# Expert rows stored from the unscaled residual, the norm's factor moved to a scale per slot, and SyncE's first expert loads issued around the first gather

## The chip, the cores and the metric

The kernel runs on one core of one Trainium2 chip. The metric is the time of one execution in device microseconds; a comparison takes the median of several. The five engines that matter here are TensorE (PE, with its weight loads PEld), VectorE (DVE), ScalarE (ACT), GpSimd (POOL) and SyncE (SP). SP, ACT and POOL also issue DMAs.

## What is computed

A two-layer model on 512 tokens of width 1024, float32 throughout. Each layer is a mixer, a cross attention and a mixture of experts, each added to the residual `h`. The change lies in the experts alone:

```python
def hier_moe(xn, w_grp, b_grp, w_exp, b_exp, w1, w3, w2):       # xn = rmsnorm(h, gain)
    ...                                   # router: a group of 4, then the best 2 of its 4 experts, w_tok
    gate = jnp.sum(jax.nn.one_hot(eid, N_EXPERTS) * w_tok[..., None], axis=1)
    hid = jax.nn.silu(jnp.einsum('td,edf->tef', t, w1)) * jnp.einsum('td,edf->tef', t, w3)
    hid = hid * gate[..., None]
    y = hid.reshape(t.shape[0], N_EXPERTS * EXP_FF) @ w2.reshape(N_EXPERTS * EXP_FF, dm)
```

`rmsnorm(h, g)` is `h * rstd * g`, with one `rstd` per token. There are 16 experts, w1 and w3 are 1024 x 256, w2 is 256 x 1024.

## The kernel before

Every engine runs one hand-written program; the order on an engine is the order of its code, and engines meet at semaphores. A layer's experts work on items: an item is one expert with 128 slots for token rows. With these inputs there are 16 items in a layer, four quads of four.

**The rows.** After the cross attention `h` lies in SBUF as four tiles of 128 tokens. ACT's `norm` squares each tile (L1466), then `experts` on ACT scales it by `rstd` into `xn` (L1723, in the buffer `E`) and stores it to the DRAM tensor `xs` (L1727). The semaphore `xs_stored` counts these four stores. POOL gathers an item's rows from `xs` by an indirect DMA (L699) into one of two buffers, PE turns them (L1153), and ACT and DVE split them into high and low parts (L1751, L2423). Item 0 takes another way: PE picks its rows out of `xn` with a one-hot matrix (`first_rows`, L1115).

**The router.** DVE computes it in one long row of small instructions (L2295 to L2398), most of which wait for the one before. In it are the slots of each token (`slots_ready`, on which POOL's first gather waits), the gates (L2368, L2369), and a one-hot product that brings the gates to the slots (`item_gate`, L2370 and L2372, PE's L1137, and the copy L2398 to `gslot`). Behind it DVE splits item 1's up weights (L2412) and rows (L2419, L2423); PE's `up` of item 1 (L1175, then L1185) needs them.

**An item.** `up` (both up projections in one 512-column bank), `turn_hidden` (L1197), `turn` (L1153, of the rows two items ahead) and `down` (L1214) on PE; on ACT the silu L1756, the high parts of the weights (L1743, L1763), and the copies of the result to `yo` (L1795); on DVE the product with the gate (L2404) and the low parts. ACT takes an item's up weights (L1743) two items before PE uses them.

**The loads.** SP loads the weights: `load_up` (2048 KB, L542) and `load_down` (1024 KB, L545) into four slots each, and stores the results of items 0 to 12 to `ybuf` (L551); all are on SP's one DMA queue. For items 0 to 3 the order is written out; from item 4 on a load waits until its slot is free. In layer 0 the queue ends with a 2048 KB panel of layer 1 and the store of item 12. Then POOL gathers rows of `ybuf` back into `h` (L726, eight times, adding), DVE adds the last three items, which PE brings to tokens (L1237, added at L2478), and layer 1 starts with PE turning `h` (L783).

Of the kernel before, what the change touches and what calls it, by code (L numbers as in the profile page):

```python
# [28 lines left out]
ALU = mybir.AluOpType  # L29
# [49 lines left out]
def program(nc, A, out):  # L79
# [19 lines left out]
    with ctx:  # L99
# [226 lines left out]
        xn = v3(E[0], 4)  # L326

# [136 lines left out]
        item_gates = st[:, 232:236]  # L464
# [29 lines left out]
        def c3(ap):  # L494
# [15 lines left out]
        item_gate = v3(E4, 8, 1536, 1536 + 8 * NI)  # L510
        LATE = 3
        slot_of_row, tile_row, late_tok, gslot = [
            sm[:, lo:lo + n] for lo, n in ((592, 4 * LATE), (604, 4), (611, LATE), (616, NI))]
# [12 lines left out]
        def _(sp):  # L526
# [8 lines left out]
            def experts(l):  # L535
# [19 lines left out]
                for j in range(2):  # L555
                    load_up(NE * l + j, j)
                    load_down(NE * l + j, j)
                    if j == 0:
                        sp.wait_ge(S["xs_stored"], 16 * TT * (l + 1))
                load_up(NE * l + 2, 2)  # L560
                await_filled(sp, first[f"route{l}"])
                load_down(NE * l + 2, 2)
                sp.wait_ge(m["xt_filled"], 2)
                sp.wait_ge(m["xg_in1"], 16)
# [59 lines left out]
        def _(pool):  # L624
# [56 lines left out]
            def experts(l):  # L681
# [7 lines left out]
                def gather(q, j):  # L689

                    par = j % 2
                    if not isinstance(q, int) or j >= 2:

                        wait_alone(m["xt_filled"], q * (2 * SLOTS) + (2 * j - 2))
                    if not isinstance(q, int):
                        pool.tensor_copy(item_gates[:, j:j + 1], gslot[:, bass.ds(q * SLOTS + j, 1)])  # L696
                    pool.tensor_copy(idx[:, par:par + 1], slots[:, bass.ds(q * SLOTS + j, 1)]).then_inc(m["idx_ready"], 1)
                    wait_alone(m["idx_ready"], q * SLOTS + j)
                    pool.indirect_dma_start(xg[par], None, xs[l],  # L699
                                            bass.IndirectOffsetOnAxis(ap=idx[:, par:par + 1], axis=0),  # L700
                                            bounds_check=T - 1, oob_is_err=False)\
                        .then_inc(m[f"xg_in{par}"], 16)
# [70 lines left out]
        def _(pe):  # L773
# [300 lines left out]
            def experts(l):  # L1074
# [33 lines left out]
                pe.wait_ge(S["xs_rows"], TT * (l + 1))  # L1108
# [3 lines left out]
                def first_rows(b, k0, k1):  # L1112
                    for k in range(k0, k1):
                        for t in range(TT):
                            ins = pe.matmul(banks[b][:, k * P:(k + 1) * P], xn[:, t, (4 * b + k) * P:(4 * b + k + 1) * P],  # L1115
                                            first1h[:, t, :], start=(t == 0), stop=(t == TT - 1))
                    if k1 == 4:
                        ins.then_inc(m["xt_filled"], 1)
# [12 lines left out]
                def slot_gates():  # L1131

                    u = first[f"gslot{l}"]
                    claim(pe, u)
                    pe.wait_ge(S["onehots_ready"], 2 * l + 2)
                    for n in range(2 * TT):
                        ins = pe.matmul(bank(u)[:, 0:NI], slot1h[:, n, :].bitcast(F32), item_gate[:, n, :], start=(n == 0),  # L1137
                                        stop=(n == 2 * TT - 1))
                    fill(ins, u)
# [281 lines left out]
        def _(act):  # L1421
# [34 lines left out]
            def squares(name, t0=0, t1=TT):  # L1456

                n = NORMS[name]
                for t in range(t0, t1):
                    h_is_ready(name, t)  # L1460
                    if name == "mix_norm0":
                        dst = memV[:, t % MT, :]
                        act.wait_ge(S["stat_ready"], t + 1)
                    else:
                        dst = E[3 if name == "mix_norm1" else 1][:, t * D:(t + 1) * D]
# [251 lines left out]
            def experts(l):  # L1717
                m = M[l]
                norm(f"ffn_norm{l}")
                act.wait_ge(S["rstd_ready"], 3 * l + 2)  # L1720
                for t in range(TT + 1):
                    if t < TT:
                        act.activation(xn[:, t, :], h[:, t, :], ACT.Copy,  # L1723
                                       scale=rstd[:, NORMS[f"ffn_norm{l}"], t:t + 1]).then_inc(S["xs_rows"], 1)
                    if t > 0:
                        act.wait_ge(S["xs_rows"], TT * l + t)
                        act.dma_start(xs[l][(t - 1) * P:t * P, :], xn[:, t - 1, :]).then_inc(S["xs_stored"], 16)  # L1727
# [25 lines left out]
                def gated_hidden(q, j):  # L1753

                    act.wait_ge(m["hid_filled"], q * SLOTS + (j + 1))
                    act.activation(silu[j % 2], banks[2 + j % 2][:, 0:FF], ACT.Silu).then_inc(m["silu_ready"], 1)  # L1756
# [216 lines left out]
        def _(dve):  # L1973
# [306 lines left out]
            def experts(l):  # L2280
# [89 lines left out]
                v(tt(item_gate, mid(iof[:, 0:NI], 8), last(itemf, NI), ALU.is_equal))  # L2370
                gates = gate[:, :, :].rearrange("p j t -> p (j t)")
                v(tt(item_gate, item_gate, last(gates, NI), ALU.mult), "onehots_ready")  # L2372
# [25 lines left out]
                evac(dve.tensor_copy(gslot, bank(u)[:, 0:NI]), u)  # L2398

                def hidden(q, j):  # L2400
                    par = j % 2
                    dve.wait_ge(m["silu_ready"], q * SLOTS + (j + 1))
                    gate_ = gslot[:, j:j + 1] if isinstance(q, int) else item_gates[:, j % SLOTS:j % SLOTS + 1]
                    stt(hid[par], silu[par], gate_, banks[2 + par][:, FF:2 * FF], ALU.mult, ALU.mult).then_inc(m["hid_ready"], 1)  # L2404
# [370 lines left out]
```

## Time and profile before

| | |
|---|---|
| median of 3 runs | 1171.49 us (1171.18 to 1172.44) |
| the profiled execution | 1168.69 us, span 1166.9 us |
| busy shares of the span | PE 97%, DVE 62%, ACT 57%, POOL 31% |
| granted TensorE clock, mean | 0.990 |
| experts, layer 0 | from 378 us to 575 us of the span |
| experts, layer 1 | from 965 us to the end |

The page's shares are means over very different stages. In the experts one item takes 9.87 us, and in that stretch PE, DVE, ACT and the DMA engines are all busy over 90% of the time. So the views to read are those that show order: the chain that ended last, the timelines of PE and SP at the start of the experts, and the time from a DMA's issue to its landing. The start of the experts in layer 1 repeats that of layer 0 about 587 us later.

### The profile page before, as it was taken

The numbers are of one execution on the slowest core, as the hardware profiler recorded it, in microseconds if no ns is written. First come the engines' busy times: TensorE is split into PE (matmuls) and PEld (weight loads), VectorE is DVE, ScalarE is ACT, GpSimd is POOL, SyncE is SP. The second block draws the span as 40 slices with busy tenths as digits, with TensorE's granted clock in tenths as the row PEclk, the third lists the DMA queues.
The fourth block names the chain that finished last, engine by engine and source line by source line (L and its number), as shares of the span: only waits on it lengthen the run. The fifth ranks groups of instructions, "written<-read, shape, count | busy, mean of one in ns | idle before, by whom it ended". The sixth has DMA issues, their size and how long they took to land.

```text
span 1166.9 us, 15858 instructions
## 1 busy us (share of the span) xinstructions
PE 1131.8 (97%) x5330; PEld 868.5 (74%) x5330; DVE 726.6 (62%) x1315; ACT 661.0 (57%) x1275; POOL 367.2 (31%) x343
## 2 busy tenths in 40 slices
PE   9998999999999899999999999989999998999998
PEld 5467875788778567777878887668887786677776
DVE  5896444322332899999644993682313408999996
ACT  2553256345542489999625354444365524799993
POOL 2033350564223011111636654253442130111104
PEclk9998899999999999999999999999999999999999
DMA  9524031278100999997722120011311008999968
GB/s 377 216 112 102 12 118 73 90 277 354 73 1 7 366 396 405 399 395 283 175 87 81 73 106 39 1 73 73 142 75 73 1 1 323 389 402 393 392 273 191
DMA packets 35413, 216.38 MB, mean 185 GB/s; under 512 B 9499, under 2 KB 9627, under 8 KB 23296
## 3 DMA queue, kind: packets, MB, share of 16 engines
q1 hardware_dynamic: 23024, 181.02, 40.0%
q0 software_dynamic: 9888, 27.17, 8.0%
q10 hardware_dynamic: 2432, 7.29, 1.6%
q8 instruction: 41, 0.67, 0.2%
q14 instruction: 28, 0.23, 0.1%
HBM read 191.31 MB, written 32.51 MB: 192 GB/s over the span
## 4 chain that ended last, share of the span: by engine, by line
PE 81%; DVE 11%; DMA 3%; ACT 3%; issue 2%; SPq 0%; DVEq 0%; ACTq 0%
PE bank L832 39%; PE bank L1185 12%; PE bank L1214 8%; DMA E<-in_xt 2%; PE bank L1033 2%; PE bank L1055 2%; PE bank L1175 2%; PE bank L1237 2%; PE bank L805 1%; PE bank L994 1%; PE bank L937 1%; DVE E L2088 1%; DVE E2r L2438 1%; DVE E L2086 1%; DVE E L2087 1%
## 5 line engine op out<-in xcount | busy, mean ns | idle before, releaser
L661 POOL TENSOR_TENSOR wlo<-W,whi 128x512 fp32r<-128x512 f32 x176 | 257.1, 1481 | 422.6 <-ACT whi L1444 422.1
L1444 ACT ACTIVATE whi<-W 128x512 fp32r<-128x512 f32 x176 | 108.5, 631 | 240.4 <-PE bank L832 236.3
L832 PE MATMUL bank<-whi,xTr 128*128 128x512 f32 x480 | 193.5, 403 | 0.9 <-ACT E L1936 0.7
L832 PE MATMUL bank<-wlo,xTr 128*128 128x512 f32 x416 | 162.8, 391 | 0.0
L832 PEld LDWEIGHTS bank<-whi,xTr 128*128 128x128 f32 x480 | 90.7, 189 | 22.0 <-POOL wlo L661 1.7
L1185 PE MATMUL bank<-E4r,E1r 128*128 128x512 f32 x360 | 99.9, 426 | 0.0
L832 PE MATMUL bank<-whi,E4r 128*128 128x512 f32 x256 | 99.8, 390 | 0.0
L2038 DVE TENSOR_TENSOR h<-bank,h 128x512 f32<-128x512 f32 x32 | 21.8, 692 | 115.0 <-PE bank L832 115.0
L832 PEld LDWEIGHTS bank<-wlo,xTr 128*128 128x128 f32 x416 | 78.7, 189 | 16.7 <-issue 1.2
L1185 PEld LDWEIGHTS bank<-E4r,E1r 128*128 128x128 f32 x360 | 67.6, 188 | 27.6 <-issue 8.5
L1214 PE MATMUL bank<-whi,E2r 128*128 128x512 f32 x240 | 82.2, 404 | 3.5 <-DVE E2r L2438 1.8
L832 PE MATMUL bank<-whi,E0r 128*128 128x512 f32 x160 | 63.7, 398 | 0.0
L832 PE MATMUL bank<-whi,E2r 128*128 128x512 f32 x160 | 62.4, 390 | 0.0
L832 PE MATMUL bank<-wlo,E0r 128*128 128x512 f32 x160 | 62.2, 389 | 0.0
L696 POOL COPY st<-sm 128x1 f32 x24 | 4.4, 183 | 180.1 <-PE bank L1153 180.1
L1214 PEld LDWEIGHTS bank<-whi,E2r 128*128 128x128 f32 x240 | 45.0, 188 | 19.5 <-DVE E2r L2438 11.0
L832 PEld LDWEIGHTS bank<-whi,E4r 128*128 128x128 f32 x256 | 48.0, 188 | 10.0
L856 PE MATMUL bank<-W,E 128*128 128x512 f32 x128 | 55.4, 593 | 0.0
L1214 PE MATMUL bank<-wlo,E2r 128*128 128x512 f32 x120 | 46.8, 390 | 0.0
L856 PEld LDWEIGHTS bank<-W,E 128*128 128x128 f32 x128 | 24.2, 190 | 29.7 <-issue 29.2
L2412 DVE SCALAR_TENSOR_TENSOR E4r<-E,vectors,E4r 128x512 fp32r<-128x512 f32 x64 | 45.1, 748 | 0.0
L726 POOL DMA_INDIRECT h<-ybuf,pos x16 | 32.0, 1997 | 41.9 <-DMA ybuf<-E 37.6
(497 smaller groups left out, 2566.5 us busy)
## 6 DMA issues: line engine op xcount, KB each, us to landing
W<-in_panels SPq DMA_DIRECT2D x25, 2048.0 KB, 8.2
W<-in_up SPq DMA_DIRECT2D x16, 2048.0 KB, 13.2
E<-in_up SPq DMA_DIRECT2D x16, 2048.0 KB, 14.1
E<-in_down SPq DMA_DIRECT2D x16, 1024.0 KB, 14.7
xT<-in_down SPq DMA_DIRECT2D x16, 1024.0 KB, 15.4
ybuf<-E SPq DMA_DIRECT2D x26, 512.0 KB, 9.6
ybuf<-memV POOLq DMA_DIRECT2D x12, 1024.0 KB, 22.7
h<-in_x SPq DMA_DIRECT2D x8, 512.0 KB, 12.8
```

What stands on the lines that cost most here:

```text
L661: pool.tensor_tensor(wlo[s_ % RING][:, :], slot(name)[:, block_of(name, k), :], whi[s_ % RING][:, :].bitcast(F32), ALU.subtract).then_inc( ...
L726: pool.indirect_dma_start(h[:, t, :], None, ybuf[l], bass.IndirectOffsetOnAxis(ap=pos[:, j, t:t + 1], axis=0), bounds_check=NI * P - 1, oo ...
L832: ins = pe.matmul(bank(u + t)[:, :], a, b, start=(k == 0 and n == 0), stop=(k == KT - 1 and n == 2))
L856: ins = pe.matmul(bank(u)[:, :], memnT[:, k, t * P:(t + 1) * P], slot(f"kv{n}")[:, k, :], start=(k == 0), stop=(k == KT - 1))
L1033: ins = pe.matmul(bank(u)[:, head * NM:(head + 1) * NM], qT[:, k, t * P:(t + 1) * P], memKT[:, k, :], start=(kk == 0), stop=(kk == 1))
L1055: ins = pe.matmul(bank(u)[:, :], memV[:, k, n * XD + d * P:n * XD + (d + 1) * P], pT[:, n, k, :], start=(k == 0), stop=(k == 1))
L1175: pe.matmul(banks[2 + par][:, :], xgT[:, k, :], w13s[j][:, k, :], start=(k == 0), stop=False)
L1185: ins = pe.matmul(banks[2 + par][:, :], a, b, start=False, stop=(c == SPLIT - 1 and n == 2))
L1214: ins = pe.matmul(banks[5 + half][:, :], a, b[:, :], start=(k == 0 and n == 0), stop=(k == 1 and n == 2))
L1237: ins = pe.matmul(banks[b][:, :], late1h[:, n, t * P:(t + 1) * P], y[:, half * 512:(half + 1) * 512], start=(n == 0 and part == 0), stop=( ...
L1444: act.activation(whi[s_ % RING][:, :], slot(name)[:, block_of(name, k), :], ACT.Copy).then_inc(S["w_hi"], 1)
L2412: stt(up_lo[c], w13s[nj][:, k, :], col("norm_ffn_g", 8 * l + k), up_hi[c].bitcast(F32), ALU.mult, ALU.subtract).then_inc(m["lo_parts"], 1)
```

## The change

- `norm` on ACT now stores each tile of `h` to `xs` as soon as the tile is ready, ahead of its square. The four scalings of L1723, the buffer `xn` and the stores behind them are gone. `first_rows` on PE reads `h`.
- The rows of an item are now unscaled. Where they were scaled by `rstd`, the silu takes `rstd` of its slot as its scale, and the gate of a slot becomes gate times `rstd`. DVE builds both per token and item (`item_scale`), PE brings both to the slots in one product of 48 columns where there were 24, and `scale_of` picks the column.
- SP's first loads, written out for items 0 to 3, stand in another order and behind other waits.

```diff
                 sp.wait_ge(S["spare_rows"], 16 * 2 * (NI - NE + SLOTS) * P // NM)
-                for j in range(2):
-                    load_up(NE * l + j, j)
-                    load_down(NE * l + j, j)
-                    if j == 0:
-                        sp.wait_ge(S["xs_stored"], 16 * TT * (l + 1))
+                sp.wait_ge(S["xs_stored"], 16 * TT * (l + 1))
+                load_up(NE * l, 0)
+                load_up(NE * l + 1, 1)
+                load_down(NE * l, 0)
+                sp.wait_ge(m["xt_filled"], 2)
+                sp.wait_ge(m["xg_in1"], 16)
                 load_up(NE * l + 2, 2)
+                load_down(NE * l + 1, 1)
                 await_filled(sp, first[f"route{l}"])
                 load_down(NE * l + 2, 2)
-                sp.wait_ge(m["xt_filled"], 2)
-                sp.wait_ge(m["xg_in1"], 16)
                 load_up(NE * l + 3, 3)
                 load_down(NE * l + 3, 3)
...
                     h_is_ready(name, t)
+                    if "ffn" in name:
+                        act.dma_start(xs[int(name[-1])][t * P:(t + 1) * P, :], h[:, t, :]).then_inc(S["xs_stored"], 16)
...
-                act.wait_ge(S["rstd_ready"], 3 * l + 2)
-                for t in range(TT + 1):
-                    if t < TT:
-                        act.activation(xn[:, t, :], h[:, t, :], ACT.Copy,
-                                       scale=rstd[:, NORMS[f"ffn_norm{l}"], t:t + 1]).then_inc(S["xs_rows"], 1)
-                    if t > 0:
-                        act.wait_ge(S["xs_rows"], TT * l + t)
-                        act.dma_start(xs[l][(t - 1) * P:t * P, :], xn[:, t - 1, :]).then_inc(S["xs_stored"], 16)
...
-                    act.activation(silu[j % 2], banks[2 + j % 2][:, 0:FF], ACT.Silu).then_inc(m["silu_ready"], 1)
+                    act.activation(silu[j % 2], banks[2 + j % 2][:, 0:FF], ACT.Silu, scale=scale_of(q, j, 1)).then_inc(m["silu_ready"], 1)
...
-                v(tt(item_gate, mid(iof[:, 0:NI], 8), last(itemf, NI), ALU.is_equal))
+                row_rstd = rstd[:, NORMS[f"ffn_norm{l}"], :]
+                v(tt(gate[:, :, :], gate[:, :, :], mid(row_rstd, 2), ALU.mult))
+                v(tt(item_scale[:, :, 1, :], mid(iof[:, 0:NI], 8), last(itemf, NI), ALU.is_equal))
                 gates = gate[:, :, :].rearrange("p j t -> p (j t)")
-                v(tt(item_gate, item_gate, last(gates, NI), ALU.mult), "onehots_ready")
+                v(tt(item_scale[:, :, 0, :], item_scale[:, :, 1, :], last(gates, NI), ALU.mult))
+                for j in range(2):
+                    half = item_scale[:, TT * j:TT * (j + 1), 1, :]
+                    ins = tt(half, half, last(row_rstd, NI), ALU.mult)
+                v(ins, "onehots_ready")
```

On SP, where the experts of layer 0 begin (`W` and `E` with `in_up` are the slots of the up weights, `E` and `xT` with `in_down` those of the down weights), the order before was:

```order
L542 DMA W<-in_up 128x4096 [waits filled6,spare_rows,filled2]
L545 DMA E<-in_down 128x2048
L542 DMA W<-in_up 128x4096 [waits xs_stored]
L545 DMA E<-in_down 128x2048
L542 DMA E<-in_up 128x4096
L545 DMA xT<-in_down 128x2048 [waits filled7]
L542 DMA E<-in_up 128x4096 [waits xg_in1_0,xt_filled_0]
L545 DMA xT<-in_down 128x2048
```

On SP, the same eight loads after:

```order
L546 DMA W<-in_up 128x4096 [waits spare_rows,filled6,xs_stored,filled2]
L546 DMA W<-in_up 128x4096
L549 DMA E<-in_down 128x2048
L546 DMA E<-in_up 128x4096 [waits xg_in1_0,xt_filled_0]
L549 DMA E<-in_down 128x2048
L549 DMA xT<-in_down 128x2048 [waits filled7]
L546 DMA E<-in_up 128x4096
L549 DMA xT<-in_down 128x2048
```

Six loads stood ahead of the wait for the first gather's landing (`xg_in1`), now three do; the five behind it are item 2's up, item 1's and 2's down, and item 3's pair. The wait for the rows' stores (`xs_stored`) now stands ahead of all of them.

On DVE, in the router where the gates are ready (`gate` holds them, `E` the one-hots per item), the order before was:

```order
L2368 TENSOR_TENSOR gate<-sm 128x4 [waits d_step]
L2369 TENSOR_TENSOR gate<-gate,sm 128x4 [waits d_step]
L2370 TENSOR_TENSOR E<-iof,E 128x192 [waits d_step]
L2372 TENSOR_TENSOR E<-E,gate 128x192 [waits d_step]
L2374 COPY E<-iof 1x48 [waits onehots_ready]
```

On DVE, the same place after:

```order
L2366 TENSOR_TENSOR gate<-sm 128x4 [waits d_step]
L2367 TENSOR_TENSOR gate<-gate,sm 128x4 [waits d_step]
L2369 TENSOR_TENSOR gate<-gate,rstd 128x8 [waits d_step]
L2370 TENSOR_TENSOR E<-iof,E 128x8x24 [waits d_step]
L2372 TENSOR_TENSOR E<-E,gate 128x8x24 [waits d_step]
L2375 TENSOR_TENSOR E<-E,rstd 128x4x24 [waits d_step]
L2375 TENSOR_TENSOR E<-E,rstd 128x4x24
L2378 COPY E<-iof 1x48 [waits onehots_ready]
```

Three instructions are new, one of 8 columns and two of 96; nothing on DVE is taken away.

## Rows read from the trace of the kernel before

**Rows 1.** Chain that ended last, layer 0: start us, us, what.

```profile
399.66 0.69 DVE E L2286
...
412.40 0.48 DVE E1r L2423
...
412.92 1.12 PE bank L1175 x2
```

**Rows 2.** Timeline of PE: start us, us, instructions, [idle before, what ended it].

```profile
410.21 1.09 PE L1153 MATMUL bank<-ident,E 128*128 128x128 f32 x8 [0.88 <-DMA E<-xs,idx]
...
997.99 1.09 PE L1153 MATMUL bank<-ident,E 128*128 128x128 f32 x8 [1.66 <-DMA E<-xs,idx]
1000.07 1.13 PE L1175 MATMUL bank<-W,E 128*128 128x512 f32 x2 [0.99 <-DVE E1r L2423]
```

**Rows 3.** Timelines of DVE and ACT at the start of the experts, layer 0.

```profile
376.51 1.06 ACT L1466 ACTIVATE E<-h 128x1024 f32<-128x1024 f32 x1 [7.48 <-DVE h L2038]
383.92 0.34 ACTq L1727 DMA_DIRECT2D xs<-E  x1
381.02 0.16 DVE L1986 TENSOR_SCALAR ssq<-ssq 128x4 f32<-128x4 f32 x1
386.22 0.24 DVE L2305 TENSOR_TENSOR sm<-sm,vectors 128x80 f32<-128x80 f32 x1
```

**Rows 4.** Groups of instructions on ACT, shapes apart: count, busy us, mean ns.

```profile
L1743 ACT ACTIVATE E4r<-E,vectors 128x512 fp32r<-128x512 f32 x64 | 42.8, 723 | 0.0
L1763 ACT ACTIVATE whi<-E 128x512 fp32r<-128x512 f32 x64 | 35.1, 634 | 0.0
```

**Rows 5.** Timelines of SP and POOL: issues of the first loads and of the first gather.

```profile
393.66 0.33 SPq L542 DMA_DIRECT2D W<-in_up  x1
394.51 0.43 SPq L542 DMA_DIRECT2D E<-in_up  x1
400.27 1.10 POOL L699 DMA_INDIRECT E<-xs,idx  x1 [0.98 <-PE bank L1115]
```

**Rows 6.** Issue to landing, us: item 1's down, item 2's up, the first gather (layer 0).

```profile
L545 SPq DMA_DIRECT2D E<-in_down x1: 434/434/434, 394.0 to 394.0; - x1
DMA to landing us min/median/max: 9.7/9.7/9.7
DMA to landing us min/median/max: 14.7/14.7/14.7
DMA to landing us min/median/max: 9.9/9.9/9.9
```

**Rows 7.** Issue to landing, us: eight gathers L726 of layer 0; final stores of `h`.

```profile
DMA to landing us min/median/max: 5.9/7.0/8.1
DMA to landing us min/median/max: 2.6/3.6/4.4
```

**Rows 8.** By stage: us; PE, PEld, DVE, ACT, POOL busy; clock, DMA share, GB/s.

```profile
503.00:513.00 10.00, 9.94 (x47) 7.78 (x46) 9.50 (x17) 9.16 (x18) 1.33 (x3) 1.00 0.99 399
546.00:548.00 2.00, 2.00 (x15) 1.72 (x14) 2.00 (x4) 1.16 (x4) 0.00 (x0) 1.00 0.13 53
```

**Rows 9.** Layer 1: landing of item 6's up; item 15's up; ACT's first use of it.

```profile
DMA to landing us min/median/max: 13.4/13.4/13.4
L542 SPq DMA_DIRECT2D E<-in_up x1: 341/341/341, 1111.6 to 1111.6; - x1
DMA to landing us min/median/max: 18.6/18.6/18.6
1131.85 1.95 ACT L1743 ACTIVATE E4r<-E,vectors 128x512 fp32r<-128x512 f32 x3
```

**Rows 10.** Timelines of POOL, DVE and PE at the end of layer 0's experts.

```profile
550.50 1.58 POOL L726 DMA_INDIRECT h<-ybuf,pos  x1 [19.41 <-DMA ybuf<-E]
573.17 1.29 DVE L2478 TENSOR_TENSOR h<-bank,h 128x512 f32<-128x512 f32 x2 [0.91 <-DMA h<-ybuf,pos]
575.26 3.65 PE L783 MATMUL bank<-ident,h 128*128 128x128 f32 x32
```

More of the change, by code:

```diff
@@ L324, in v3 @@
             return buf[:, lo:hi].rearrange("p (a b) -> p a b", a=a)
-        xn = v3(E[0], 4)
         s5T = v3(E[0], G)
@@ L463, in program @@
         xmx, xnm, xsum, xrec = st[:, 0:16], st[:, 16:32], st[:, 32:48], st[:, 48:64]
-        item_gates = st[:, 232:236]
         wsN = v3(wsT, 4)
@@ L509, in program, with scale_of @@
         half_ = E4[:, 1920:1924]
-        item_gate = v3(E4, 8, 1536, 1536 + 8 * NI)
+        item_scale = E4[:, 3072:3072 + 16 * NI].rearrange("p (n a i) -> p n a i", n=8, a=2)
+        slot_scales = v3(sm, 2, 520, 520 + 2 * NI)
+        item_scales = v3(st, 2, 232, 232 + 8)
+        def scale_of(q, j, a):
+            return slot_scales[:, a, j:j + 1] if isinstance(q, int) else item_scales[:, a, j % 4:j % 4 + 1]
         LATE = 3
-        slot_of_row, tile_row, late_tok, gslot = [
-            sm[:, lo:lo + n] for lo, n in ((592, 4 * LATE), (604, 4), (611, LATE), (616, NI))]
+        slot_of_row, tile_row, late_tok = [
+            sm[:, lo:lo + n] for lo, n in ((592, 4 * LATE), (604, 4), (611, LATE))]
         nquad, late_from, past = E4[:, 296:297], E4[:, 297:298], E4[:, 304:312]
@@ L695, in gather @@
                     if not isinstance(q, int):
-                        pool.tensor_copy(item_gates[:, j:j + 1], gslot[:, bass.ds(q * SLOTS + j, 1)])
+                        pool.tensor_copy(item_scales[:, :, j:j + 1], slot_scales[:, :, bass.ds(q * SLOTS + j, 1)])
                     pool.tensor_copy(idx[:, par:par + 1], slots[:, bass.ds(q * SLOTS + j, 1)]).then_inc(m["idx_ready"], 1)
@@ L1107, in experts @@
                     taken(pe, max(v for v in range(u + 1) if bank_of[v] == b))
-                pe.wait_ge(S["xs_rows"], TT * (l + 1))
                 fill_wait(unused, memory_keys, 1)
@@ L1114, in first_rows @@
                         for t in range(TT):
-                            ins = pe.matmul(banks[b][:, k * P:(k + 1) * P], xn[:, t, (4 * b + k) * P:(4 * b + k + 1) * P],
+                            ins = pe.matmul(banks[b][:, k * P:(k + 1) * P], h[:, t, (4 * b + k) * P:(4 * b + k + 1) * P],
                                             first1h[:, t, :], start=(t == 0), stop=(t == TT - 1))
@@ L1136, in slot_gates @@
                     for n in range(2 * TT):
-                        ins = pe.matmul(bank(u)[:, 0:NI], slot1h[:, n, :].bitcast(F32), item_gate[:, n, :], start=(n == 0),
+                        ins = pe.matmul(bank(u)[:, 0:2 * NI], slot1h[:, n, :].bitcast(F32),
+                                        item_scale[:, n, :, :].rearrange("p a i -> p (a i)"), start=(n == 0),
                                         stop=(n == 2 * TT - 1))
@@ L2397, in experts @@
                 await_filled(dve, u)
-                evac(dve.tensor_copy(gslot, bank(u)[:, 0:NI]), u)
+                evac(dve.tensor_copy(slot_scales, bank(u)[:, 0:2 * NI].rearrange("p (a i) -> p a i", a=2)), u)
                 def hidden(q, j):
@@ L2402, in hidden @@
                     dve.wait_ge(m["silu_ready"], q * SLOTS + (j + 1))
-                    gate_ = gslot[:, j:j + 1] if isinstance(q, int) else item_gates[:, j % SLOTS:j % SLOTS + 1]
-                    stt(hid[par], silu[par], gate_, banks[2 + par][:, FF:2 * FF], ALU.mult, ALU.mult).then_inc(m["hid_ready"], 1)
+                    stt(hid[par], silu[par], scale_of(q, j, 0), banks[2 + par][:, FF:2 * FF], ALU.mult, ALU.mult).then_inc(m["hid_ready"], 1)
                 def up_low_parts(q, j, c0, c1, part):
```

## The prediction

> **What bounds the kernel now.** I read the chain that ended last first, in the two places where the experts begin, then PE's timeline there. Between the router and item 1's `up` the chain is one engine's: DVE runs from L2286 at 399.66 us to the first half of L2423 at 412.40, with nothing on the chain between but its own next instruction, and PE's L1175 starts at 412.92 the moment DVE lets it [rows 1]. PE also waits for the first gather there, 0.88 us in layer 0 and 1.66 us in layer 1 [rows 2], but what follows that gather still waits for DVE. To be seen in these rows: the wait that the change shortens, for the gather, is not the one that ends last.
>
> Then I read the stages. Inside the experts a stretch of 10 us has PE busy 9.94, DVE 9.50, ACT 9.16, and a DMA share of 0.99 at 399 GB/s [rows 8]. PE sets the pace there, but the DMA engines have nothing to spare. That is why I read the landing times last, and they decide: in layer 1 item 6's up weights land 13.4 us after their issue, item 15's 18.6 us after [rows 9]. The issues keep PE's pace, so the landings fall behind by 5.2 us in nine items, about 0.6 us for each. The queue never catches up, and whatever delay it starts with it carries to the end.
>
> **The change part by part. The rows' store.** ACT loses four scalings, and PE a wait on them that had long been met. None is on the chain, so they are worth nothing. The four issues move ahead of the squares. One took 0.34 us [rows 3]; the first stands open before the first square, the others run beside the square before them. The DVE instruction that waits for the squares started at 381.02 [rows 3], right behind DVE's own earlier work, so I take 0.2 us for a later route, with 0 and 0.35 as ends.
>
> **The scale per slot.** DVE gains one 8-column and two 96-column instructions in the chain of rows 1. A small one of the same engine took 0.16 us, an 80-column one 0.24 [rows 3]. With the step to the next instruction that makes 0.2 + 2 x 0.25 = 0.7 us per layer, 0.4 if the two run into each other, 0.8 at most. PE's product has 48 columns for 24, inside `first_up`, which ends before DVE is ready: nothing. The silu's scale becomes a column of SBUF. On ACT 512 columns took 0.723 us with such a scale and 0.634 without [rows 4], so 0.09 us per item, under an engine that is not full [rows 8]; where the last quad's chain goes through the silu it may show, 0 to 0.2 us per layer. POOL copies two columns for one: nothing. Together these make 0.7 + 0.2 = 0.9 us per layer at most places, less where one hides the other; I carry 0.85, or 1.7 us for both layers.
>
> **The loads.** Here is the large term. Before, SP restarted at 393.66 with item 1's up, and item 1's down, item 2's up and down stood right behind it [rows 5]. After, the rows are stored where the squares began, at 376.5, where their stores had begun at 383.9 [rows 3], and item 0's up, item 1's up and item 0's down follow them at about 385 us (2.1 MB of stores are 5 us at the 400 GB/s of rows 8, and some 3 us pass from issue to landing, rows 7): 5.2 MB, another 13 us. They are in before the first gather is issued at 400.27 [rows 5], so nothing that needs them waits: item 1's up comes earlier than before, item 0's down is first used once item 1's `up` runs. But the next five loads now wait until that gather has landed, and behind them on SP stand item 4's loads and all stores and loads after them. Between, the DMA engines have only the gather to move.
>
> How long is that? Under load the first gather took 9.9 us [rows 6]. On idle engines no row shows it. From below, the plain 512 KB stores at the kernel's end took 2.6 to 4.4 us, 3.6 in the middle; from above, the adding gathers of 128 full rows took 5.9 at least [rows 7]. I take 4.0, near the plain stores, as the rows are plain copies and fewer, with POOL's 1.10 us for the instruction [rows 5] in it. The gather then lands at 404.3, and the queue restarts there instead of at 393.66: 10.6 us later. It has one up and the gather less to move. Item 1's down landed at 394.03 + 9.7 = 403.7 and item 2's up at 394.51 + 14.7 = 409.2 [rows 5, 6], so an up beside the gather takes 5.5 us. **The lag is 10.6 - 5.5 = 5.1 us**, with 3.7 and 7.0 as ends (2.6 and 5.9 for the gather). Layer 1 repeats this stretch 587.15 us later (PE's L1175 at 1000.07 and 412.92) [rows 1, 2], so I take the same lag.
>
> The Trainium skill, "DMA: Bandwidth & Descriptors", section "Anatomy of one DMA — SWDGE (gpsimd) path", gives about 2.0 us plus the bytes at 436 GB/s for one DMA. For 512 KB that is an estimate of 3.2 us by that page, which the final stores bear out (2.6 to 4.4, rows 7). With it the lag would be 4.3 and the sum below 6.2 us instead of 7.8.
>
> Where does the lag come out? In layer 0 the last store is at the queue's very end. POOL waited 19.41 us for it and began at 550.50; between 546 and 548 only 0.13 of the DMA engines was still at work [rows 8, 10], so it is a few of them that finish late. Through the gathers into `h` the third tile's add ended at 573.17 + 1.29 = 574.46, having waited for its gather, and PE's L783 starts at 575.26 [rows 10]: 0.8 us of room. Layer 0 loses 5.1 - 0.8 = 4.3 us. In layer 1 item 15's up landed at 1111.6 + 18.6 = 1130.2 and ACT first read it at 1131.85 [rows 9]: 1.65 us of room, so 5.1 - 1.65 = 3.45 us, by which ACT, DVE and PE stop in the last quad. The 0.85 us of DVE in each layer lie under these: they move PE, while the loads' landing stays where it is.
>
> **Sum:** 4.3 + 3.45 = 7.75 us on the profiled 1168.69, so 1176.4. The runs shown have a median 2.8 us above that execution, so I predict 1171.49 + 7.8 = **1179.3 us**. The ends of the lag give 2.9 + 2.05 = 4.95 and 6.2 + 5.35 = 11.55 us, or 1176.4 and 1183.0.
>
> **The rivals. The lag is absorbed.** The loads of a layer are issued by free slots, and if the engines that finish late were idle at some time before the tail, the lag would end there. For it: the room of items 4 to 12 is larger than that of item 15, and the overall share of 0.99 is a mean over 16 engines. Against it: the growth of rows 9. Then only DVE's 1.7 us remain: 1173.2 us, 0.5 to 2.5 above before. This is the case of no change.
>
> **The gather's wait was the bound.** Then PE gets back 0.88 + 1.66 us, and in layer 1 the 0.99 us that follow [rows 2], 3.5 us in all: 1168.0 us, faster. It needs DVE to be free earlier; but L2412 and L2423 stand in a fixed order behind the router on DVE, and the chain has no gap for another to fill [rows 1]. It decides only if DVE's stretch shrinks by more than the 0.7 us added, for which I see no reason.
>
> **The gather stays slow.** If the three loads are still in the queue at 400 us, because the stores land late, the gather again takes up to 9.9 us [rows 6]. The lag is then 400.27 + 9.9 - 393.66 - 5.5 = 11.0 us, and the two layers lose 10.2 + 9.35 = 19.6: 1191.1 us. For it: four stores of 512 KB and three loads in some 23 us is close. Against it: they make 7.3 MB, 18 us at 400 GB/s.
>
> **How the numbers follow.** Forecast 0.62 (1176.4 to 1183.0), absorbed 0.20, gather was the bound 0.08, gather stays slow 0.10. Everything within 0.2% of before (2.3 us, about what a measurement of this kernel tells from no change) comes from the absorbed case, 0.17; its upper part, the forecast and the slow gather make slower 0.74; the gather case and a little of the absorbed one make faster 0.09. The range goes from 1172.0, the lower end of the absorbed case, to 1183.0; it leaves out the two last rivals, 0.18.
>
> **What would show it.** In the changed trace item 2's up should be issued near 404 us, and the first gather land in about 4 us. PE's wait before its first L1153 should be gone, and L1175 of item 1 should start 0.7 to 1 us later, released by DVE. The landing of item 15's up should be later by the lag in both layers, with a wait of ACT on it in layer 1; POOL's first L726 of layer 0 should start near 555.6, and DVE's L2478 wait for gathers before L783. I am wrong if the lag at item 4 is there but gone by item 12, or if item 1's `up` starts earlier than before.

## The result

The kernel after takes 1177.31 us in the median of 20 runs (1170.39 to 1185.05), the kernel before 1171.39 us of as many on the same chip: a ratio of 1.0068 on record, interval 1.0045 to 1.009, or 5.3 to 10.5 us more (the two medians alone give 1.0051, or 5.9 us). Forecast were 7.8 us more, and 1179.3.

Every kernel here, the one before included, varies over 7 to 16 us from run to run, and the longer runs have the lower mean granted clock (of before, some 0.987 at 1172 us and 0.995 at 1163 us). Unchanged stretches show it; here are two windows before the experts, first of before, then of after (us; PE, PEld, DVE, ACT, POOL busy; clock, DMA share, GB/s):

```profile
100.00:120.00 20.00, 18.18 (x126) 17.02 (x124) 6.60 (x12) 7.41 (x14) 2.42 (x2) 0.75 0.60 108
120.00:140.00 20.00, 20.00 (x74) 15.48 (x74) 7.95 (x7) 4.69 (x8) 5.19 (x3) 0.82 0.02 4
```

```profile
100.00:120.00 20.00, 18.18 (x153) 16.47 (x152) 6.61 (x12) 7.53 (x14) 2.49 (x3) 1.00 0.61 113
120.00:140.00 20.00, 20.00 (x82) 15.22 (x81) 15.78 (x10) 6.09 (x11) 13.04 (x5) 1.00 0.02 4
```

The profiled execution of after came 7.65 us sooner to the experts, through code that the change does not touch, so its span (1170.3 against 1166.9) understates the loss. I therefore count each layer from ACT's first square of the experts' norm. In before that is at 376.51 [rows 3] and in layer 1 at 963.51; in after at 368.86 and 962.61, the first row being before's, the others after's (ACT timelines):

```profile
963.51 1.06 ACT L1466 ACTIVATE E<-h 128x1024 f32<-128x1024 f32 x1 [7.48 <-DVE h L2038]
```

```profile
368.86 1.06 ACT L1472 ACTIVATE E<-h 128x1024 f32<-128x1024 f32 x1 [7.86 <-DVE h L2036]
962.61 1.06 ACT L1472 ACTIVATE E<-h 128x1024 f32<-128x1024 f32 x1 [7.85 <-DVE h L2036]
```

From there layer 0 ends (PE's last turn of `h`) at 202.40 in before (575.26 + 3.65, [rows 10]) and 207.32 in after (574.43 + 1.75, below): **4.92 us more**. Layer 1 takes 203.39 to the end of the span in before and 207.69 in after: **4.30 us more**. Between the layers, in unchanged code, after took 1.83 us longer: PE stood still for 2.79 us at 784 us of the span, and the clock behind it was 0.62 for 3 us, where before kept 1.00 behind the same pause of 2.86 us. The sum is 4.92 + 4.30 + 1.83 - 7.65 = 3.4, the difference of the spans.

### The profile page after: what moved, and what is told of

It is laid out like the page before. It is cut to its first block, busy times and chain, and to the rows that moved or that the text cites. A ratio compares the mean times of both kernels' runs of the same rounds, so it can differ in the third digit from the quotient of the medians.

```text
span 1170.3 us, 15854 instructions
## 1 busy us (share of the span) xinstructions
PE 1128.9 (96%) x5330; PEld 863.8 (74%) x5330; DVE 728.4 (62%) x1321; ACT 655.2 (56%) x1267; POOL 366.6 (31%) x343
## 4 chain that ended last, share of the span: by engine, by line
PE 69%; DVE 13%; ACT 6%; DMA 6%; issue 4%; POOL 0%; SPq 0%; ACTq 0%; DVEq 0%; POOLq 0%
PE bank L836 39%; PE bank L1189 7%; PE bank L1218 4%; DMA E<-in_xt 2%; PE bank L1037 2%; PE bank L1059 2%; DMA h<-ybuf,pos 2%; DVE E4r L2415 2%; DVE wlo L2435 2%; ACT uhi L1741 1%; PE bank L1179 1%; PE bank L809 1%; PE bank L998 1%; DVE E L2086 1%; ACT E L1793 1%
## 5 line engine op out<-in xcount | busy, mean ns | idle before, releaser
L1189 PE MATMUL bank<-E4r,E1r 128*128 128x512 f32 x360 | 102.9, 436 | 0.0
L700 POOL COPY st<-sm 128x2 f32 x24 | 4.5, 186 | 187.1 <-PE bank L1157 187.1
L1741 ACT ACTIVATE E4r<-W,vectors 128x512 fp32r<-128x512 f32 x56 | 37.2, 722 | 15.7 <-DVE sm L2402 15.7
```

What stands on the lines that cost most here:

```text
L1189: ins = pe.matmul(banks[2 + par][:, :], a, b, start=False, stop=(c == SPLIT - 1 and n == 2))
L1741: act.activation(up_hi[c], w13s[nj][:, NATIVE + c, :], ACT.Copy, scale=col("norm_ffn_g", 8 * l + NATIVE + c))\
```

## The profile after

PE where item 1 begins, first in before's layer 0, then in after's layer 0 and layer 1 (timeline; answers to [rows 2]), and after's windows around that place in layer 0:

```profile
412.92 1.12 PE L1175 MATMUL bank<-W,E 128*128 128x512 f32 x2 [1.62 <-DVE E1r L2423]
```

```profile
401.32 1.04 PE L1157 MATMUL bank<-ident,E 128*128 128x128 f32 x8
405.89 1.69 PE L1179 MATMUL bank<-W,E 128*128 128x512 f32 x2 [3.53 <-DVE E1r L2426]
406.60 4.80 PE L1189 MATMUL bank<-E4r,E1r 128*128 128x512 f32 x12
...
999.76 1.64 PE L1179 MATMUL bank<-W,E 128*128 128x512 f32 x2 [3.66 <-DVE E1r L2426]
```

```profile
398.00:402.00 4.00, 4.00 (x21) 2.52 (x21) 3.54 (x14) 1.49 (x3) 0.00 (x0) 1.00 0.88 295
402.00:405.80 3.80, 0.36 (x4) 0.12 (x2) 3.80 (x8) 3.77 (x7) 2.16 (x3) 1.00 0.92 377
405.80:408.80 3.00, 2.91 (x6) 1.75 (x7) 3.00 (x7) 1.99 (x4) 0.00 (x0) 0.59 1.00 422
408.80:412.00 3.20, 3.20 (x14) 2.59 (x13) 2.37 (x4) 2.14 (x3) 0.00 (x0) 0.85 1.07 451
```

PE no longer waits for the gather. But the wait for DVE that was 1.62 us in before is now 3.53 us in one piece, and behind it the clock is 0.59 for 3 us, so most of that window is at its lower level of 1.2 GHz: L1179 takes 1.69 us for 1.12. That I had not foreseen.

The transfers, issue to landing in us. Layer 0's last store in before:

```profile
542.97 0.35 SPq L551 DMA_DIRECT2D ybuf<-E  x1
DMA to landing us min/median/max: 6.6/6.6/6.6
```

In after the first gather of layer 0 and of layer 1, item 2's up, layer 0's last store, and item 15's up in layer 1:

```profile
DMA to landing us min/median/max: 4.1/4.1/4.1
DMA to landing us min/median/max: 4.2/4.2/4.2
...
396.62 0.33 SPq L546 DMA_DIRECT2D E<-in_up  x1
DMA to landing us min/median/max: 9.9/9.9/9.9
...
L555 SPq DMA_DIRECT2D ybuf<-E x1: 351/351/351, 538.0 to 538.0; - x1
DMA to landing us min/median/max: 9.9/9.9/9.9
...
L546 SPq DMA_DIRECT2D E<-in_up x1: 341/341/341, 1113.0 to 1113.0; - x1
DMA to landing us min/median/max: 19.5/19.5/19.5
```

The gather lands in 4.1 us, against 9.9 [rows 6]. The last store lands at 547.9, 179.0 us behind the first square; in before it landed at 549.6, 173.1 behind. **The lag at the queue's end is 5.9 us.**

What it does to layer 0's end (timelines of DVE and PE; answers to [rows 10]), and DVE's waits in layer 1's last third, first in before, then in after (us in total, times, longest):

```profile
566.87 1.29 DVE L2481 TENSOR_TENSOR h<-bank,h 128x512 f32<-128x512 f32 x2 [4.21 <-DMA h<-ybuf,pos]
573.09 1.29 DVE L2481 TENSOR_TENSOR h<-bank,h 128x512 f32<-128x512 f32 x2 [1.20 <-DMA h<-ybuf,pos]
572.04 2.16 PE L787 MATMUL bank<-ident,h 128*128 128x128 f32 x18 [1.68 <-DVE h L2481]
574.43 1.75 PE L787 MATMUL bank<-ident,h 128*128 128x128 f32 x14 [0.24 <-DVE h L2481]
```

```profile
DVE h L2478 <- PE bank L1237: 4.0, 3, 1.4
```

```profile
DVE h L2481 <- DMA h<-ybuf,pos: 5.5, 4, 2.2
```

In both layers DVE's last adds now wait for gathers into `h`, and in layer 0 PE for them; in before those of layer 1 waited for PE.

## The experiments

Times below are counted from the layer's first square, in each kernel's profiled execution: the start of item 1's `up`, the turn of item 0's hidden rows (L1197 before, L1201 after), the end of the layer. The ratios are to the kernel before on the same chip. One execution gives each row's layer times, so they need not add up to its ratio: they do within the interval, but for e2's and e3's: these lose 12.2 and 8.2 us in the two layers, where their intervals end at 11.8 and 7.4 us.

| kernel | layer 0: up, hidden, end | layer 1: up, hidden, end | median us | ratio (interval) |
|---|---|---|---|---|
| before | 36.41, 42.23, 202.40 | 36.56, 42.38, 203.39 | | |
| after | 37.03, 44.47, 207.32 | 37.15, 44.57, 207.69 | 1177.31 | 1.0068 (1.0045 to 1.009) |
| e1, old order | 37.04, 44.38, 204.60 | 37.17, 45.89, 206.99 | 1175.09 | 1.0044 (1.0011 to 1.0077) |
| e2, new order alone | 36.42, 43.84, 209.65 | 37.60, 45.01, 208.34 | 1175.21 | 1.0068 (1.0034 to 1.0101) |
| e3, free loads | 37.05, 45.56, 206.77 | 37.37, 46.05, 207.17 | 1173.67 | 1.0031 (0.9999 to 1.0063) |
| e4, six products | 38.49, 44.21, 206.49 | 38.49, 44.18, 205.55 | 1177.77 | 1.0054 (1.0024 to 1.0084) |
| e5, three products | 37.04, 42.86, 208.53 | 37.16, 42.98, 204.68 | 1173.39 | 1.005 (1.0021 to 1.0078) |
| e6, old order, two products | 37.04, 42.85, 203.02 | 37.16, 43.00, 204.08 | 1168.25 | 1.000 (0.9972 to 1.0027) |
| e7, second gather awaited | 37.04, 42.85, 209.20 | 37.18, 42.96, 205.65 | 1175.14 | 1.008 (1.0052 to 1.0107) |
| e8, free loads, three products | 37.04, 42.85, 203.40 | 37.18, 42.96, 204.00 | 1168.00 | 1.0003 (0.9975 to 1.0031) |
| e9, doubled lag | 37.04, 42.86, 212.08 | 37.16, 42.97, 208.81 | 1176.78 | 1.0101 (1.0059 to 1.0143) |
| e10, table on POOL | 36.04, 41.83, 202.34 | 36.04, 41.83, 203.09 | 1165.97 | 0.9982 (0.9954 to 1.001) |

### One part at a time: e1, e2, e3

The theory was the prediction's: the lag of SP's queue carries the loss. The rival: the scale per slot does. **e1** gives the changed kernel SP's old order:

```diff
-                sp.wait_ge(S["xs_stored"], 16 * TT * (l + 1))
-                load_up(NE * l, 0)
-                load_up(NE * l + 1, 1)
-                load_down(NE * l, 0)
-                sp.wait_ge(m["xt_filled"], 2)
-                sp.wait_ge(m["xg_in1"], 16)
-                load_up(NE * l + 2, 2)
-                load_down(NE * l + 1, 1)
+                for j in range(2):
+                    load_up(NE * l + j, j)
+                    load_down(NE * l + j, j)
+                    if j == 0:
+                        sp.wait_ge(S["xs_stored"], 16 * TT * (l + 1))
+                load_up(NE * l + 2, 2)
                 await_filled(sp, first[f"route{l}"])
                 load_down(NE * l + 2, 2)
+                sp.wait_ge(m["xt_filled"], 2)
+                sp.wait_ge(m["xg_in1"], 16)
                 load_up(NE * l + 3, 3)
```

> The changed kernel with SP's eight first loads in the order and behind the waits of before; the stores of h and the scale per slot stay. Theory (the lag of SP's queue carries the loss): item 2's up is issued near 386 us less than 1 us behind before, item 4's up and the last store land within 1 us of before, the first POOL gather into h starts within 1 us of before, and only DVE's 0.8 us per layer is left, so the median is 0 to 1.7 us above before. Rival (the scale on DVE and ACT is the loss): the median stays where the changed kernel's is, about 6 to 8 us above before. With the loads under the gather again, PE's idle time before item 1's up should be in two pieces and the granted clock behind it 1.00.

The lag was gone (layer 0's last store at 172.4), yet layer 0 ended 2.2 us and layer 1 3.6 us behind before: neither theory. PE's rows of both layers, and the window there in layer 1, tell why:

```profile
412.49 2.08 PE L1179 MATMUL bank<-W,E 128*128 128x512 f32 x2 [3.04 <-DVE E1r L2426]
...
1003.48 2.08 PE L1179 MATMUL bank<-W,E 128*128 128x512 f32 x2 [2.51 <-DVE E1r L2426]
```

```profile
1003.40:1010.40 7.00, 6.92 (x16) 4.78 (x17) 5.13 (x10) 4.23 (x7) 0.39 (x2) 0.55 1.02 428
```

Ahead of these waits PE had waited for the gather too, 0.28 us in layer 0 and 0.93 in layer 1:

```profile
408.36 1.09 PE L1157 MATMUL bank<-ident,E 128*128 128x128 f32 x8 [0.28 <-DMA E<-xs,idx]
...
999.87 1.09 PE L1157 MATMUL bank<-ident,E 128*128 128x128 f32 x8 [0.93 <-DMA E<-xs,idx]
```

So the idle time was in two pieces, as in before, but the longer one was 3.04 and 2.51 us where before's was 1.62 and 1.66: the gather landed 0.8 to 1.0 us sooner, and DVE came 0.6 us later. The clock behind it was 0.55 in layer 1, and L1179 took 2.08 us for 1.12 in both. My expectation of a clock of 1.00 was wrong, and the whole loss of layer 1 stands already at item 0's hidden rows (45.89 against 42.38).

**e2** is the kernel before with the changed order of SP, the reverse of the diff above:

> The kernel before with SP's eight first loads in the order and behind the waits of the change, nothing else; the stores still follow the four scalings. Theory (the lag carries the loss): the queue restarts when the first gather has landed, some 10 us later than before, and the median is 4 to 9 us above before; somewhat more than in the changed kernel if the loads ahead of the gather, which wait for later stores here, still slow the gather. Rival (the scale is the loss): within 1 us of before.

The order alone costs as much as the whole change: 7.25 us in layer 0, 4.95 in layer 1. A part of the 7.25 us is a second pause, at the layer's end: PE waited there 3.77 us for DVE and the gathers, and turned `h` in 5.32 us for 3.65. The scale isn't in this kernel, and the lower clock is there all the same:

```profile
411.54 1.50 PE L1175 MATMUL bank<-W,E 128*128 128x512 f32 x2 [2.73 <-DVE E1r L2423]
```

So the lower clock does not need the scale; that it comes from PE's idle time is what e4 and e5 test.

**e3** moves the wait for the gather three loads back, with the early stores kept:

```diff
                 load_down(NE * l, 0)
-                sp.wait_ge(m["xt_filled"], 2)
-                sp.wait_ge(m["xg_in1"], 16)
                 load_up(NE * l + 2, 2)
                 load_down(NE * l + 1, 1)
                 await_filled(sp, first[f"route{l}"])
                 load_down(NE * l + 2, 2)
+                sp.wait_ge(m["xt_filled"], 2)
+                sp.wait_ge(m["xg_in1"], 16)
                 load_up(NE * l + 3, 3)
```

> The changed kernel with item 2's up and items 1's and 2's down ahead of the wait for the first gather, as many loads ahead of it as before, but all behind the early stores of h. Theory (lag): the queue starts earlier than before's and has no gap, so the loads from item 4 on land no later than before's, and the median is 1 us below to 1.7 us above before. The gather is slow again (8 to 10 us), so if the early gather was what matters (rival), the loss or gain should show at item 1's up: later than in the changed kernel by 1 us or more and the median above before by 2 us or more.

The first store of results lands at 54.3, 2.1 us ahead of before's, and the gather at 32.0, as slow as expected; item 1's `up` starts where after's does, so the early gather bought nothing. But PE's idle time is 3.54 us, and its clock is lower for longer than in after: the hidden rows come 3.33 us behind before. The leading loads could not help a PE that was late itself.

### The clock by itself: e4, e5, e6, e8

**e4** fills PE's idle time, in the changed kernel, with products into a bank that nothing uses there:

```diff
                 first_up()
                 turn(0, 1)
+                fill_wait(5, memory_keys, 6)
```

> The changed kernel with six more products of 128x512 on PE into an unused bank (0.54 us each) between the turn of item 1's rows and its up, where PE is idle for 3.5 us. Rival (the lower granted clock behind that idle time is the loss): item 1's up goes from 7.4 to 5.8 us, and the median falls by 2 to 3.5 us, 1.6 us per layer. Theory (lag): the loads land where they did, so in layer 0 nothing comes of it, in layer 1 0 to 1.6 us: the median falls by 0 to 1.6 us.

Six were too many (PE timeline): each product is two passes, and together they took 5.32 us and delayed the `up` by 1.4 us.

```profile
410.17 5.32 PE L815 MATMUL bank<-memKT,ident 128*128 128x512 f32 x12
415.32 1.02 PE L1179 MATMUL bank<-W,E 128*128 128x512 f32 x2
```

Yet the `up` was fast again, and item 0's hidden rows came 0.26 us ahead of after's. Layer 1 gained 2.1 us; the medians can't tell (a ratio of 1.0054, for 1.0068 of after). **e5** has three products:

> The changed kernel with three more products of 128x512 on PE (0.89 us each, as the run with six showed) between the turn of item 1's rows and its up, so that the idle time of 3.5 us is filled by 2.7 and the up isn't delayed. Theory (two costs that don't add in layer 0: the lag of the loads and the lower granted clock): item 1's up starts as in the changed kernel, 37.0 us behind the first square, at a granted clock of 1.00, and item 0's hidden rows are turned 0.6 us behind before's instead of 2.2. Layer 0 still ends 4 to 5 us behind before, since the gathers into h end it; layer 1 ends 0.6 to 2.7 us behind before instead of 4.3. Rival (the lag alone, in both layers): layer 1's end stays 4 us behind.

PE's rows in layer 0, then DVE's waits in the last adds of layer 0 and of layer 1:

```profile
402.11 2.74 PE L815 MATMUL bank<-memKT,ident 128*128 128x512 f32 x6
405.82 1.12 PE L1179 MATMUL bank<-W,E 128*128 128x512 f32 x2 [0.96 <-DVE E1r L2427]
```

```profile
DVE h L2482 <- DMA h<-ybuf,pos: 8.3, 4, 5.6
...
DVE h L2482 <- PE bank L1241: 4.0, 3, 1.4
```

This separates the causes. The `up` starts where it did and is at full clock; hidden rows come 1.6 us sooner in both layers. Layer 1 gains 3.0 us and ends 1.29 behind before, as expected. Layer 0 ends 6.1 us behind before, where I had expected 4 to 5. Its adds wait 8.3 us for gathers, and DVE's last add ends 205.6 us behind the square, as in after (205.5), so the lag sets that. But PE, early and then idle in one piece, turns `h` slowly:

```profile
571.96 5.35 PE L787 MATMUL bank<-ident,h 128*128 128x128 f32 x32 [3.29 <-DVE h L2482]
```

Before's turn took 3.65 us [rows 10]. In e5 it ends 2.9 us behind DVE's last add, in after, whose PE had waited 1.68 us, 1.8: some 1.1 us of e5's layer 0 are the clock again (0.70 over 3 us there). **e6** is e1 with two products:

> The changed kernel with SP's loads in the order of before, and two products of 128x512 on PE (1.8 us) in the idle time of 2.5 to 3.0 us ahead of item 1's up. Theory: with the lag undone and the clock kept, only DVE's 0.6 us per layer is left; layer 0 ends 0.6 us behind before, layer 1 0.6 us, and the median is 1 to 2 us above before. Rival (something else in the scale per slot costs time in the items): both layers stay 2 us or more behind.

Both layers come out 0.62 and 0.69 us behind before, the ratio is 1.000, and DVE's adds wait for PE as in before's layer 1. That is DVE's part of the change, and nothing of the scale is left over. e5 and e6 differ in SP's order and in one product, and their items run within 0.4 us of each other in layer 0; so the two show how far a lag is carried. e5's loads land 7.0 us after e6's at item 2, 5.1 at item 4, 7.2 at item 15, and the last store 5.9 (178.7 against 172.8 behind the square; its issue and landing in e5, then in e6):

```profile
L555 SPq DMA_DIRECT2D ybuf<-E x1: 350/350/350, 536.3 to 536.3; - x1
DMA to landing us min/median/max: 11.2/11.2/11.2
```

```profile
L555 SPq DMA_DIRECT2D ybuf<-E x1: 350/350/350, 544.0 to 544.0; - x1
DMA to landing us min/median/max: 5.6/5.6/5.6
```

Over 130 us nothing of it is made up: 5 to 7 us throughout. In layer 1 the loads come as late, 5.2 us at item 2, 8.2 at item 4 and 8.4 at item 15, but the last store only 3.8. e5 minus e6 is the price of SP's order with the clock at item 1 held: **5.5 us in layer 0, 0.6 us in layer 1**. Of the 5.5 us the lag is 4.8 at DVE's last add (205.6 against 200.9); the rest is PE's slow turn. **e8** is e3 with three products:

> The changed kernel with as many loads ahead of the wait for the gather as before, behind the early stores, and the three products on PE. Theory: the loads lead before's at item 4 and stay level with PE behind it, the clock stays at 1.00, and both layers end 0.6 us behind before (layer 0 0 to 0.6, as its last adds then wait less for gathers): the median is 0 to 1.2 us above before. Rival (loads ahead of the gather slow it until it is last): item 1's up starts more than 1 us behind the changed kernel's.

It ends 1.0 and 0.6 us behind before (in layer 0 a little more than the 0 to 0.6 expected): most of e3's loss was the clock.

### The lag by itself: e7, e9

Both start from e5. **e7** adds a wait for the second gather:

```diff
                 sp.wait_ge(m["xg_in1"], 16)
+                sp.wait_ge(m["xg_in0"], 16)
                 load_up(NE * l + 2, 2)
```

> The changed kernel with the three products on PE, and SP waiting for the second gather too before item 2's up: that gather lands 2.6 us after the first. Theory (the lag is carried to the end): item 4's up, the last store and the gathers into h of layer 0 come about 2.6 us later than with the three products alone, and layer 0 ends 2.6 us later (2 to 3.2); layer 1 0 to 2.6 us later. Rival (the loads of a layer wait for free slots and absorb a lag): the end of layer 0 moves by less than 1 us.

SP restarted 2.1 us later, but item 2's up landed in 8.0 us instead of 9.9:

```profile
DMA to landing us min/median/max: 8.0/8.0/8.0
```

The second gather had only been moved out of its way. The loads were 0.2 us later there and layer 0's last store not at all; the 0.67 us by which layer 0 ended later lie in the gathers behind it. This tells nothing for or against the theory, since no idle time was added to the queue. **e9** adds some, by a wait for PE's turn of item 1's rows:

```diff
-                sp.wait_ge(m["xt_filled"], 2)
+                sp.wait_ge(m["xt_filled"], 4)
                 sp.wait_ge(m["xg_in1"], 16)
```

> The changed kernel with the three products on PE, and SP waiting, before item 2's up, not only for the first gather but for PE's turn of its rows: that stands behind first_up and ends 5.8 us after the gather has landed, and between the DMA engines have only the second gather to move. (Waiting for that second gather had moved the loads by only 0.2 to 0.8 us, since they no longer shared the engines with it.) Theory (a gap of the queue is carried to the end): item 4's up and layer 0's last store land 4 to 5.5 us later than with the three products alone, and layer 0 ends that much later; layer 1, whose room is used up, 3 to 5 us later; the median 7 to 10 us above that run's. Rival (lags are absorbed inside a layer): less than 2 us in each.

Item 2's up landed 3.4 us later than in e5 (41.1 against 37.8 behind the square), layer 0's last store 3.5 (182.3 against 178.7), and layer 0 ended 3.55 us later, layer 1 4.13. The gap was not the 4 to 5.5 us that I had expected, since the second gather moved in it. ACT's waits for weights at the first items of layer 0 and of layer 1, then DVE's in the last adds of layer 1:

```profile
ACT E4r L1742 <- DMA E<-in_up: 4.5, 2, 2.3
...
ACT E4r L1742 <- DMA E<-in_up: 4.6, 2, 2.6
```

```profile
DVE h L2482 <- DMA h<-ybuf,pos: 5.8, 4, 2.5
```

More lag costs as much more, in both layers now. But the items themselves stopped for it and ran some 3 us later from the third on, so their slots came free later too: this run shows the price of more lag, not that a queue with time to catch up would keep it. For that e5 and e6 stand.

### What bounds item 1: e10

If DVE bounds item 1's `up`, a shorter stretch of DVE must start it sooner, even with a slow gather. In e8, with one product for three, part of DVE's table of spare items goes to POOL, and a comparison into the 0.67 us in which DVE waits for PE:

```diff
+                v(tt(b1, mid(cum[0:1, :], 8), last(iof[0:1, 1:9], NE * NX), ALU.is_equal))
                 turn(0, 0, 1)
...
-                v(dve.tensor_copy(c3(epx), last(iof[0:1, 0:NE], NX)))
-                v(ts(nth, iof[0:1, 0:8], 1.0, None, ALU.add))
-                v(tt(b1, mid(cum[0:1, :], 8), last(nth, NE * NX), ALU.is_equal))
-                v(tt(b1, b1, mid(more[0:1, :], 8), ALU.mult))
-                v(tt(b2, b1, mid(epx, 8), ALU.mult))
-                v(dve.memset(tabf, 0.0))
-                v(dve.tensor_copy(tabf[:, 0:NE], iof[0:1, 0:NE]))
+                dve.wait_ge(S["xs_rows"], 3 * l + 3)
```

> The kernel with more loads ahead of the gather, with one product in PE's idle time instead of three, and DVE's table of spare items shortened: four of its instructions go to POOL, one is left out by a merge of two, and the comparison is made ahead of the router's end, in the 0.67 us in which DVE waits for PE. DVE's stretch ahead of item 1's rows is 2.6 us shorter. Theory (that stretch bounds item 1's up, the gather doesn't): the up starts earlier until PE's turn of the rows is last, 1.0 to 2.0 us ahead of the same kernel without this, at 35.0 to 36.0 us behind the first square; each layer ends 0.3 to 1.4 us ahead of before. Rival (the gather or PE bounds it): the up moves by less than 0.3 us.

The gather landed as late as in e8 (32.0), and the `up` started 1.00 us sooner in layer 0 and 1.14 in layer 1: DVE bounds it, the gather doesn't. Both are at the lower end of what I expected, and the layers ended ahead of before by 0.06 and 0.30 us only, where I had expected 0.3 to 1.4. It has the lowest ratio of the kernels here, with the early stores in it; but 0.9982 has 1 inside its interval. Timelines of DVE and POOL show what ate a part of the 2.6 us:

```profile
394.76 1.03 DVE L2386 TENSOR_TENSOR E<-E,gate 128x192 f32<-128x192 f32 x1
...
394.36 1.21 POOL L719 TENSOR_TENSOR E<-E 1x384 f32<-1x384 f32 x1
```

DVE's 192-column product took 1.03 us beside POOL's, where it took 0.36 in e8; its comparison of 192 columns just before, at 394.36, took 0.36 though POOL's product had begun. DVE then waited 0.46 us for PE's product of the slots' scales.

## Why the prediction came out

**The gather.** Forecast 4.0 us on free engines, measured 4.1 and 4.2 in the two layers. By the Trainium skill, "DMA: Bandwidth & Descriptors", section "Anatomy of one DMA — SWDGE (gpsimd) path", the estimate was 3.2 us; the runs here say more.

**The lag.** Forecast 5.1 us (3.7 to 7.0), measured 5.9 at layer 0's last store. Its way through the last store, the gathers and DVE's adds to PE was the one forecast, and layer 0 lost 4.92 us (4.3 forecast). e5 and e6 give 4.8 for it at DVE's last add, and show it carried. What PE does sooner or later lies under it, as forecast of DVE's part: DVE's last add ends at 205.6 in e5 and 205.5 in after, though e5's items run 1.6 us sooner. The sign that the forecast took for a queue that never catches up, landings 5.2 us later over nine items, is weaker than it looked: in layer 0 of the same trace they fall behind by 1.8 us (12.6 to 14.4), in e6's layer 1 by 0.7 (10.8 to 11.5). What is carried is e5 against e6. With the 7.65 us of the unchanged stretch added, SP issued item 2's up at 404.3 (forecast near 404) and POOL's first gather into `h` began at 556.4 (forecast 555.6).

**DVE's new instructions.** Forecast 0.85 us per layer, measured 0.62 and 0.59 at item 1's `up`. The pair of 96 columns took 0.43 us. The silu costs what was forecast (lines of after, then of before, by shape; count, busy us, mean ns):

```profile
L1754 ACT ACTIVATE E<-bank,sm 128x256 f32<-128x256 f32 x10 | 4.7, 471 | 0.0
```

```profile
L1756 ACT ACTIVATE E<-bank 128x256 f32<-128x256 f32 x32 | 12.1, 380 | 6.1 <-PE bank L1185 6.1
```

It is 0.091 us more each, and e6 shows that little of it reaches the end: it is 0.62 us behind before at item 0's hidden rows and 0.62 at the end of layer 0, 0.62 and 0.69 in layer 1.

**Layer 1 came out near by luck.** This is the step that failed: "In layer 1 item 15's up landed at 1130.2 and ACT first read it at 1131.85: 1.65 us of room, so 5.1 - 1.65 = 3.45". In after it landed at 1113.0 + 19.5 = 1132.5, only 3.2 us later against the first square, and ACT, itself 2.3 us later, never waited for it. Before's own queue had slowed in layer 1 (18.6 us to landing, [rows 9]; 11.5 in e6), so a part of the lag was there already. The measured 4.30 us are 0.59 of DVE, 1.60 of the clock (from `up` to hidden rows 7.42 us for 5.82), and 2.1 behind the hidden rows, in the gathers into `h`, for which DVE's last adds wait. So the lag does cost something in layer 1, but through these gathers. From item 0's hidden rows to the end it takes 161.0 to 161.3 us in the kernels without the lag (before, e1, e3, e6, e8, e10), and 161.4 to 163.3 in those with it (after, e2, e4, e5, e7): the lag is worth 0.1 to 2.3 us there, 0.6 by e5 and e6. What differs between after (163.1) and e4 (161.4), with the same loads, is mostly POOL: its instructions for the first four of the eight gathers took 10.0 us in after and 8.4 in e4, and the eighth gather landed at 202.9 us behind the square, in e4 at 200.3. Why POOL took longer stays open.

**What was missing.** I named 1.62 us of PE waiting for DVE, and 0.88 for the gather, and said the second goes. I did not ask what one idle time of 3.5 us does to PE behind it. In after's layer 0 it costs nothing, since the lag covers it; in layer 1 it is 1.6 us, and up to 2.9 in e1. And where PE was kept early and then met the lag (e5, e7, e9), a pause of 3.3 to 3.9 us came at layer 0's end in its place, and turning `h` took 5.2 to 5.4 us for 3.65.

**The rivals.** Absorption falls by e5 and e6 in layer 0. That the gather's wait was the bound falls by e3 and e10. The gather did not stay slow: SP's three loads had landed by 391.1 us, ahead of its issue at 392.43.

## What to carry to other kernels

Here the DMA engines were full for a whole stage, and an idle gap made for one urgent transfer at its start was paid again at its end, 130 us later. Before making such a gap, ask first whether that transfer is the last of what its reader waits for. When a wait of TensorE grows or moves, look at the clock behind it: three products into an unused bank cost nothing here (six were too many) and show within one run what the clock was worth. And trace each layer's end for itself: the lag was worth some 5 us in the layer whose last store came 6 us later, and 0.1 to 2.3 us in the other.

## What the runs showed of the hardware

- At the start of item 1, in the twelve profiled executions, the granted clock behind PE's wait fell to its lower level all eight times when the longest piece of idle time was 2.51 to 3.66 us (after, e1, e2, e3, both layers), and was 1.00 all sixteen times when it was 1.66 us or less (before, and the kernels with products in it). How long it stayed low differed: item 1's `up` until hidden rows took 7.4 us in after, 8.7 in e1's layer 1, and 5.8 at full clock. In sum the idle time was 2.50 and 2.65 us in before and 2.73 in e2's layer 0, so these runs do not show that the longest piece is what matters.
- The length of a pause alone doesn't tell: behind one in unchanged code (first of before, then of after) the clock was 1.00 in before and, after 3.14 us, in e10, and 0.50 to 0.74 over 3 us in the ten others, after 2.65 to 3.06 us.

```profile
787.27 1.37 PE L1367 MATMUL bank<-ident,E 128*128 128x128 f32 x10 [2.86 <-ACT E L1906]
784.45 1.68 PE L1371 MATMUL bank<-ident,E 128*128 128x128 f32 x10 [2.79 <-ACT E L1904]
```

- A transfer that was given idle engines gained nothing for those behind it: the gather went from 9.9 to 4.1 us, and layer 0's last store came 5.9 us later.
- One DVE product of two SBUF operands took 1.03 us beside an instruction of POOL, where it takes 0.36 without. The Trainium skill, "GPSIMD Engine Reference", section "1. Specifications", says that the two share SBUF interfaces and contend when a DVE instruction has two SBUF inputs. This row fits that, but the comparison before it, also of two SBUF operands and beside the same POOL instruction, was not slower, so the cause is not shown.
